# Expert tiles of a mixture-of-experts layer: pad slots are left out of the gathers and of the result writes, and the results go to token order

## The chip, the core and the metric

One core of one Trainium2 chip runs the whole program. The metric is the device time of one execution in microseconds (us), as the median of several executions.

## The reference, cut to what matters

Two layers of a transformer trunk work on 384 tokens (128 of a prompt, 256 latent ones) of width 1024, all in float32. Each layer has a token-mixing half (four parallel mixers, gates, projections) and then a mixture of experts. Only the second is touched by the change:

```python
scores = jax.nn.sigmoid((t @ lp['w_router']).astype(jnp.float32))
...
_, eidx = lax.top_k(masked, TOP_K)                 # 4 of 32 experts for each token
w = jnp.take_along_axis(scores, eidx, axis=-1)
w = w / jnp.sum(w, axis=-1, keepdims=True) * ROUTE_SCALE
combine = jnp.sum(jax.nn.one_hot(eidx, N_EXPERTS, dtype=jnp.float32) * w[..., None], axis=1)
gu = jnp.einsum('nd,edf->nef', t, lp['w_exp_gu'])
a = jax.nn.silu(gu[..., :EXPERT_FF]) * gu[..., EXPERT_FF:]
a = (a * combine[..., None].astype(a.dtype)).reshape(-1, N_EXPERTS * EXPERT_FF)
routed = a @ lp['w_exp_down'].reshape(N_EXPERTS * EXPERT_FF, D_MODEL)
```

A shared expert is added for every token, and the sum goes through an RMS norm, a gate and a residual add.

## The kernel before

A loop over the two layers holds one block in which every engine has its own program; semaphores tie them together. Data of the expert stage:

- 384 tokens choose 4 experts each: 1536 choices (`CHOICES`), 48 for an expert on average. Choices are laid out in *tiles* of `CAP` = 96 slots that belong to one expert. There are `NT` = 48 tiles at most; an expert with more than 96 choices gets a second one. The trace has 64 tiles over two layers, so each expert has one. Half of the slots of a layer's 32 tiles hold no choice; they are *pads*.
- The number of a slot is worked out for each choice on VectorE (`slot_u`, 12 columns: 3 token blocks times 4 choices). GpSimd scatters the token numbers to a table in DRAM, `slot_tokens`, by 12 indirect DMAs (L823), and reads it back whole into SBUF as `tokens` (L826). A table constant fills the pads with the numbers 0 to 95, so a pad fetches a real row that nobody needs.
- For each tile GpSimd copies one column of the table to `index` (L833) and issues an indirect DMA that gathers 96 rows of 4 KB from `token_rows` to `xg` (L836). Two tile buffers alternate (`e` = 0, 1).
- TensorE, for one step of a tile (the loop `steps`): transposes the rows of the tile two ahead (L1940), gate-and-up product of the tile one ahead (L1670, 16 matmul records), transposes the activated product of its own tile (L1903), and down product of its own tile (L1670, 8 records). ScalarE (L1175 to L1185) and VectorE (L1638, L1566, L1643) empty PSUM. The results land in `yrow`.
- SyncE (SP) issues the weights of the experts, 2 MB (L657) and 1 MB (L660) for each tile, and `write_rows` (L689): 96 rows of 4 KB to `y_slots`, at the slots' places, pads included. ScalarE and VectorE wait on `y_written` before they fill the same `yrow` buffer again, two tiles later.
- After the last tile GpSimd waits for both `y_written` and gathers the results by 12 indirect DMAs of 128 rows (L856), one for each token block and choice, into six buffers `ybuf`. VectorE adds each to `acc` with its weight (L1652), and after each fourth one (the next block's second is done first) runs the norm and residual of a block (`residual`, L1493 to L1495). The next layer starts behind that.
- Slots beyond tile 32 are zeroed ahead of time: a memset (L800) and a 6 MB DMA from GpSimd (L802), in the gate stage.

Every chunk of the layer runs in the order in which it is written for its engine; nothing is scheduled at run time. Two places are serial for the whole core: the hand-over from routing to the first tile (VectorE, 12 scatters, table, gather, TensorE), and the end of a layer (last result, write, gathers, sums).

## Time and profile before

| what | value |
|---|---|
| time, median of 3 runs | 2414.11 us (2413.77 to 2420.31) |
| profiled execution: first to last instruction | 2406.7 us |
| median time less that span | 7.4 us |
| TensorE busy | 2112.7 us (88%) |
| VectorE / ScalarE / GpSimd busy | 843.8 / 641.6 / 283.2 us |
| DMA moved | 455.49 MB, 189 GB/s over the span |
| DMA issues in the expert stage | 64 of 2 MB, 64 of 1 MB, 64 result writes of 384 KB, 64 gathers |

The profiled execution has no time of its own beside its span; the 7.4 us are what a run has outside its first and last instruction. Busy time is a share of the whole span, and the stages differ much. In the expert stages (about 770 to 1167 us and 1970 to 2361 us from the start) both TensorE and the DMA engines show tenths of 9 and above, so which of the two sets the pace has to be read from what TensorE waits for.

### The profile page before, as it was taken

Reading aid. Unit: us, or ns where it says so; the run is one execution under the profiler, and the core shown is the slowest. Engines: PE = TensorE matmul, PEld = TensorE weight load, DVE = VectorE, ACT = ScalarE, POOL = GpSimd, SP = SyncE. Lnnn points to the kernel's source line nnn. Section 1 sums busy time; section 2 is a strip of 40 time slices with the busy share of each in tenths; the row PEclk is TensorE's granted clock in tenths of the full one; section 3 lists DMA queues with packets and bytes.
Section 4 is the critical chain, followed back from the end, with each engine's and each line's share of the span. In section 5 each row is a group of like instructions: output and inputs, shape, how many; then the busy total and the mean of one; then the engine's idle time right before and its main releaser. Section 6 shows DMA issues by size and latency. Waiting matters only on the chain. (4 is left out here: it accounts for less than half of the span.)

```text
span 2406.7 us, 24752 instructions
## 1 busy us (share of the span) xinstructions
PE 2112.7 (88%) x8386; PEld 1283.7 (53%) x8386; DVE 843.8 (35%) x1476; ACT 641.6 (27%) x1330; POOL 283.2 (12%) x318
## 2 busy tenths in 40 slices
PE   6999898999976999999379998989999769999992
PEld 1298666788763333333113886667887523333330
DVE  0224466544444111111412345665444531111114
ACT  1133246433240111111111332474333401111111
POOL 0000420400003000000200006104000020000002
PEclk9999999999987999999789999999999889999996
DMA  9643210363333799999495432104533439999984
GB/s 312 224 138 127 84 36 1 104 206 123 131 132 105 271 329 326 328 327 321 163 310 192 150 124 74 36 1 150 178 123 114 154 92 313 326 331 322 332 292 168
DMA packets 205619, 455.49 MB, mean 189 GB/s; under 512 B 18668, under 2 KB 29260, under 8 KB 205524
## 3 DMA queue, kind: packets, MB, share of 16 engines
q1 hardware_dynamic: 174592, 384.86, 46.9%
q0 software_dynamic: 17216, 58.84, 7.3%
q10 hardware_dynamic: 13720, 10.60, 1.4%
q8 instruction: 54, 0.88, 0.2%
q14 instruction: 37, 0.30, 0.0%
HBM read 409.63 MB, written 44.68 MB: 189 GB/s over the span
## 5 line engine op out<-in xcount | busy, mean ns | idle before, releaser
L1670 PE MATMUL psum<-W,zf 128*96 128x512 f32 (+1 forms) x1584 | 715.1, 601 | 43.8 <-ACT zf L1181 41.0
L1670 PEld LDWEIGHTS psum<-W,zf 128*96 128x96 f32 (+1 forms) x1584 | 251.9, 166 | 413.0 <-issue 356.0
L1718 PE MATMUL psum<-W_split,qT_split 128*128 128x512 f32 (+3 forms) x1536 | 410.4, 379 | 6.9 <-ACT hT L909 6.6
L1268 DVE TENSOR_TENSOR W_split<-W,W_split 128x2048 fp32r<-128x2048 f32 (+3 forms) x96 | 221.3, 2307 | 428.1 <-ACT W_split L937 428.1
L1718 PEld LDWEIGHTS psum<-W_split,qT_split 128*128 128x128 f32 x1536 | 283.9, 189 | 62.5 <-ACT hT L909 7.3
L937 ACT ACTIVATE W_split<-W 128x2048 fp32r<-128x2048 f32 (+3 forms) x96 | 175.7, 1838 | 489.5 <-PE psum L1718 360.3
L1718 PE MATMUL psum<-W_split,scratch_split 128*128 128x512 f32 x864 | 281.0, 397 | 0.7 <-DVE hT_split L1263 0.7
L1670 PE MATMUL psum<-W,silT 128*2 128x512 f32 x384 | 169.9, 605 | 76.6 <-DMA W<-in_w_mod 76.6
L1718 PE MATMUL psum<-W_split,hT_split 128*128 128x512 f32 x576 | 214.8, 400 | 5.8 <-DVE scratch_split L1456 5.8
L1718 PEld LDWEIGHTS psum<-W_split,scratch_split 128*128 128x128 f32 x864 | 162.4, 189 | 39.8 <-DVE hT_split L1263 1.1
L1566 DVE TENSOR_TENSOR zf<-psum,zf 96x256 f32<-96x256 f32 x64 | 26.9, 421 | 433.8 <-ACT zf L1179 416.7
L1718 PE MATMUL psum<-W_split,kT_split 128*128 128x512 f32 (+3 forms) x480 | 177.3, 369 | 0.0
L1670 PEld LDWEIGHTS psum<-W,silT 128*2 128x2 f32 x384 | 32.8, 86 | 212.7 <-issue 207.4
L1179 ACT ACTIVATE zf<-psum 96x256 f32<-96x256 f32 x62 | 23.5, 379 | 419.8 <-PE psum L1670 419.8
L1718 PEld LDWEIGHTS psum<-W_split,hT_split 128*128 128x128 f32 x576 | 109.9, 191 | 32.1 <-DVE scratch_split L1456 6.3
L1643 DVE COPY zf<-psum 96x512 f32<-96x512 f32 x64 | 44.0, 687 | 236.4 <-PE psum L1670 236.4
L1718 PEld LDWEIGHTS psum<-W_split,kT_split 128*128 128x128 f32 x480 | 91.1, 190 | 14.9
L1670 PE MATMUL psum<-kT,qT 64*128 64x384 f32 (+3 forms) x288 | 90.7, 477 | 5.8 <-ACT qT L973 2.8
L1940 PEld LDWEIGHTS psum<-const,zf 96*128 96x128 f32 x512 | 52.0, 147 | 63.9 <-issue 38.1
L1940 PE MATMUL psum<-const,zf 96*128 96x96 f32 x512 | 56.4, 256 | 27.9 <-DMA zf<-token_rows,vm 22.7
L833 POOL COPY vm<-vm 96x1 uint32 (+1 forms) x64 | 11.5, 180 | 579.1 <-PE psum L1940 573.8
L1341 DVE TENSOR_REDUCE nmax<-psum 128x1 f32<-128x128 f32 (+1 forms) x144 | 65.0, 465 | 39.2 <-PE psum L1670 37.5
(280 smaller groups left out, 2067.8 us busy)
## 6 DMA issues: line engine op xcount, KB each, us to landing
W<-in_w_exp_gu SPq DMA_DIRECT2D x64, 2048.0 KB, 9.5
W<-in_w_exp_down SPq DMA_DIRECT2D x64, 1024.0 KB, 9.4
W<-in_w_in SPq DMA_DIRECT2D x60, 1024.0 KB, 5.0
W<-in_w_mod SPq DMA_DIRECT2D x24, 2048.0 KB, 9.8
y_slots<-zf SPq DMA_DIRECT2D x64, 384.0 KB, 9.5
W<-in_w_br SPq DMA_DIRECT2D x16, 1024.0 KB, 4.9
y_slots<-kT POOLq DMA_DIRECT2D x2, 6144.0 KB, 32.8
W<-in_w_out SPq DMA_DIRECT2D x8, 1024.0 KB, 4.9
```

Of the source, the lines that this page charges most:

```text
L833: nc.gpsimd.tensor_copy(index[0:CAP, e:e + 1], col).then_inc(S[f"index_copied{e}"], 1)
L937: nc.scalar.activation(high(j), piece(SPLITS[j]), ACT.Copy).then_inc(S["high_ready"], 1)
L1179: nc.scalar.activation(silu[0:CAP, 1 - e, :], psum[0:CAP, BANK_GU + 1 - e, 0:FF], ACT.Silu).then_inc(S["silu_ready"], 1)
L1268: V.tensor_tensor(piece(SPLITS[j], Wr), piece(SPLITS[j]), high(j).bitcast(F32), ALU.subtract).then_inc(S["low_ready"], 1)
L1341: V.tensor_reduce(nmax[:, col:col + 1], bank(key, P * len(keys_of(t))), AX, ALU.max, negate=True).then_inc(S["max_ready"], 1)
L1566: V.tensor_tensor(av[0:CAP, s], psum[0:CAP, gu, FF:2 * FF], silu[0:CAP, s], ALU.mult).then_inc(S["dve_emptied"], 1)
L1643: V.tensor_copy(yrow[0:CAP, e, C:], psum[0:CAP, BANK_Y + 1, :]).then_inc(S["dve_emptied"], 1)
L1670: ins = nc.tensor.matmul(dst, lhsT, rhs, start=(i == 0), stop=(i == len(pairs) - 1))
L1718: ins = nc.tensor.matmul(bank(job, piece_size(key)[1]), act_part[:, k0 + k, t * P:(t + 1) * P], w_part[:, k, :], start=first and (k, i) == ...
L1940: ins = nc.tensor.transpose(psum[:, BANK_XT + h, k * CAP:(k + 1) * CAP], xg[0:CAP, s, (4 * h + k) * P:(4 * h + k + 1) * P], ident[0:CAP, 0 ...
```

## The change

The table in DRAM now holds *places*: token number times 4 plus the choice's rank. A pad holds 262144. SBUF gets `places`, and VectorE makes `tokens` of it by a shift (262144 becomes 65536). The gather has `bounds_check` 383 and the result write is an indirect DMA with `bounds_check` 1535, both without an error, so a slot beyond the bound is left out. Results go to `y_rows` in token order, 4 rows of 4 KB for each token, and are read back as six plain DMAs of 1 MB, issued by SP: for a token block, two neighbouring rows of each token. The zeroing and its DMA are gone. `xg` is cleared once in each layer, since pads are no longer written. `y_written` gets its first count from two small DMAs to `y_spare`, where SP raised it before.

```diff
-        ybuf = zf[:, 7680:13824].rearrange("p (s n) -> p s n", s=6)
+        ybuf = zf[:, 7680:13824].rearrange("p (s k n) -> p s k n", s=3, k=2)
...
-        tokens = vm[:, 1068:1068 + NT].bitcast(U32)
+        place_f = vm[:, 1556:1568]
+        places = vm[:, 1068:1068 + NT].bitcast(U32)
         index = vm[:, 1120:1122].bitcast(U32)
+        place_u = vm[:, 1488:1500].bitcast(U32)
+        tokens = vm[:, 1500:1500 + NT].bitcast(U32)
+        place_index = vm[:, 1552:1554].bitcast(U32)
...
-                    def write_rows(turn, e, less=(0, 0)):
-
-                        sp.wait_ge(*job_emptied(turn, e, "y0", less[0]))
-                        sp.sem_inc(S["sp_steps"], 1)
-                        sp.wait_ge(*job_emptied(turn, e, "y1", less[1]))
-                        sp.sem_inc(S["sp_steps"], 1)
-                        dst = a["y_slots"].rearrange("(p i) n -> p i n", i=NT)[:, bass.ds(turn * 2 + e, 1), :].rearrange("p o n -> p (o n)")
-                        sp.dma_start(dst, yrow[0:CAP, e, :]).then_inc(S[f"y_written{e}"], 16)
...
@@ -700,13 +691,19 @@
                                 load_gate_up(1 - e, expert("w_exp_gu", expert_of(tile + 3)))
                             sp.wait_ge(*job_filled(turn, e, "y1"))
                             load_down(e, expert("w_exp_down", expert_of(tile + 2)))
-                            write_rows(turn, e)
 
                     with sp.Fori(0, turns - 2) as turn:
                         steps(turn)
                     steps(turns - 2, last=True)
                     for e in range(2):
-                        write_rows(turns - 1, e, (LESS["act"][e], LESS["dve"][e]))
+                        sp.wait_ge(S[f"y_written{e}"], turns * 16 + 16)
+                        sp.sem_inc(S["sp_steps"], 1)
+                    for i in range(T * TOPK // 2):
+                        if i >= 3:
+                            sp.wait_ge(S["summed"], 2 * (i - 2))
+                        t, k = divmod(2 * i, TOPK)
+                        src = a["y_rows"].rearrange("(t p k) n -> t p k n", t=T, k=TOPK)[t, :, k:k + 2, :]
+                        sp.dma_start(ybuf[:, i % 3], src).then_inc(S[f"y_landed{i % 3}"], 16)
...
-                    nc.gpsimd.memset(zero_row, 0.0).then_inc(S["zeros_ready"], 1)
-                    pool.wait_ge(S["zeros_ready"], 1)
-                    pool.dma_start(a["y_slots"].rearrange("(p i) n -> p i n", i=NT)[:, NE:, :],
-                                   zero_row[0:CAP, None, :].to_broadcast([CAP, NT - NE, D])).then_inc(S["zeros_out"], 16)
...
                     pool.wait_ge(*filled(("R", T - 1)))
                     nc.gpsimd.memset(ones, 1.0).then_inc(S["ones_ready"], 1)
+                    pool.wait_ge(S["ones_ready"], 1)
+                    for e in range(2):
+                        pool.dma_start(a["y_spare"][e:e + 1, :], ones[0:1, :]).then_inc(S[f"y_written{e}"], 16)
...
                     pool.wait_ge(*filled(("mgT", KD // 2)))
-                    pool.wait_ge(S["zeros_out"], 16)
...
                     for i in range(T * TOPK):
-                        pool.indirect_dma_start(a["slot_tokens"], bass.IndirectOffsetOnAxis(ap=slot_u[:, i:i + 1], axis=0),
-                                                token_u[:, i // TOPK:i // TOPK + 1], None).then_inc(S["slots_out"], 16)
+                        pool.indirect_dma_start(a["slot_places"], bass.IndirectOffsetOnAxis(ap=slot_u[:, i:i + 1], axis=0),
+                                                place_u[:, i:i + 1], None).then_inc(S["slots_out"], 16)
+                    nc.gpsimd.memset(xg[0:CAP], 0.0).then_inc(S["x_cleared"], 1)
                     pool.wait_ge(S["slots_out"], 16 * T * TOPK)
-                    pool.dma_start(tokens[0:CAP], a["slot_tokens"].rearrange("(p i) o -> p (i o)", i=NT)).then_inc(S["table_in"], 16)
-                    pool.wait_ge(S["table_in"], 16)
+                    pool.dma_start(places[0:CAP], a["slot_places"].rearrange("(p i) o -> p (i o)", i=NT)).then_inc(S["table_in"], 16)
+                    pool.wait_ge(S["x_cleared"], 1)
+                    pool.wait_ge(S["tokens_ready"], 1)
                     pool.wait_ge(S["rows_out"], 16 * T)
 
                     def gather(tile, e, n):
@@ -834,8 +830,24 @@
                         pool.wait_ge(S[f"index_copied{e}"], n)
                         pool.sem_inc(S["gathers"], 1)
                         pool.indirect_dma_start(xg[0:CAP, e, :], None, a["token_rows"],
-                                                bass.IndirectOffsetOnAxis(ap=index[0:CAP, e:e + 1], axis=0)).then_inc(S[f"x_landed{e}"], 16)
-
+                                                bass.IndirectOffsetOnAxis(ap=index[0:CAP, e:e + 1], axis=0),
+                                                bounds_check=T * P - 1, oob_is_err=False).then_inc(S[f"x_landed{e}"], 16)
+
+                    def scatter(turn, e, less=(0, 0)):
+
+                        pool.wait_ge(*job_emptied(turn, e, "y0", less[0]))
+                        pool.sem_inc(S["gathers"], 1)
+                        pool.wait_ge(*job_emptied(turn, e, "y1", less[1]))
+                        nc.gpsimd.tensor_copy(place_index[0:CAP, e:e + 1], places[0:CAP, bass.ds(turn * 2 + e, 1)]
+                                              ).then_inc(S[f"place_copied{e}"], 1)
+                        pool.wait_ge(S[f"place_copied{e}"], turn + 3)
+                        pool.sem_inc(S["gathers"], 1)
+                        pool.indirect_dma_start(a["y_rows"], bass.IndirectOffsetOnAxis(ap=place_index[0:CAP, e:e + 1], axis=0),
+                                                yrow[0:CAP, e, :], None,
+                                                bounds_check=CHOICES - 1, oob_is_err=False).then_inc(S[f"y_written{e}"], 16)
+
...
                             pool.wait_ge(*job_filled(turn, e, "xt1"))
                             gather(turn * 2 + e + 4, e, turn + 3)
-
+                            scatter(turn, e)
                     for e in range(2):
-                        pool.wait_ge(S[f"y_written{e}"], turns * 16 + 16)
-                        pool.sem_inc(S["gathers"], 1)
-                    for i in range(T * TOPK):
-                        if i >= 6:
-                            pool.wait_ge(S["summed"], i - 5)
-                        pool.indirect_dma_start(ybuf[:, i % 6, :], None, a["y_slots"],
-                                                bass.IndirectOffsetOnAxis(ap=slot_u[:, i:i + 1], axis=0)).then_inc(S[f"y_landed{i % 6}"], 16)
+                        scatter(turns - 2, e)
+                    for e in range(2):
+                        scatter(turns - 1, e, (LESS["act"][e], LESS["dve"][e]))
...
-                    for t in range(T):
-                        ins = V.tensor_scalar(token_f[:, t:t + 1], const[:, K_POS + 3:K_POS + 4], float(t * P), None, ALU.add)
+                    for i in range(T * TOPK):
+                        ins = V.tensor_scalar(place_f[:, i:i + 1], const[:, K_POS + 3:K_POS + 4], float(TOPK), float(i // TOPK * P * TOPK + i % TOPK),
+                                              ALU.mult, ALU.add)
                     link(ins)
-                    V.tensor_copy(token_u, token_f)
+                    V.tensor_copy(place_u, place_f)
                     V.tensor_copy(slot_u, slot_f).then_inc(S["slots_ready"], 1)
...
+                    dve.wait_ge(S["table_in"], 16)
+                    V.tensor_scalar(tokens[0:CAP], places[0:CAP], 2, None, ALU.logical_shift_right).then_inc(S["tokens_ready"], 1)
...
                     post_gains(1)
                     for i in range(T * TOPK):
-                        dve.wait_ge(S[f"y_landed{i % 6}"], 16 * (i // 6 + 1))
-                        V.scalar_tensor_tensor(acc[:, i // TOPK], ybuf[:, i % 6], weight[:, i:i + 1], acc[:, i // TOPK], ALU.mult,
+                        dve.wait_ge(S[f"y_landed{i // 2 % 3}"], 16 * (i // 6 + 1))
+                        V.scalar_tensor_tensor(acc[:, i // TOPK], ybuf[:, i // 2 % 3, i % 2], weight[:, i:i + 1], acc[:, i // TOPK], ALU.mult,
                                                ALU.add).then_inc(S["summed"], 1)
                         dve.wait_ge(S["summed"], i + 1)
...
-    no_tokens = np.ascontiguousarray(np.broadcast_to(np.arange(CAP, dtype=np.uint32)[:, None], (CAP, NT)))
+    no_places = np.full((CAP, NT), TOPK << 16, np.uint32)
...
-    a["y_slots"] = nc.dram_tensor("y_slots", (CAP * NT, D), F32, kind="Internal").ap()
-    a["slot_tokens"] = nc.dram_tensor("slot_tokens", (CAP * NT, 1), U32, kind="Internal").ap()
+    a["y_spare"] = nc.dram_tensor("y_spare", (2, P), F32, kind="Internal").ap()
+    a["y_rows"] = nc.dram_tensor("y_rows", (CHOICES, D), F32, kind="Internal").ap()
+    a["slot_places"] = nc.dram_tensor("slot_places", (CAP * NT, 1), U32, kind="Internal").ap()
```

On GpSimd's queue, the loop over turns and what follows it. Before (from the first tile of a turn; `zf` holds `xg` and `ybuf`, `vm` the index columns; ISA and REGISTER_ALU rows are waits and counters):

```order
L833 ISA
L833 COPY vm<-vm 96x1
L834 REGISTER_ALU
L836 DMA zf<-token_rows,vm 96x1024
L847 REGISTER_ALU
L833 ISA
L833 COPY vm<-vm 96x1
L836 DMA zf<-token_rows,vm 96x1024
L845 ISA
L845 COMPARE_AND_BRANCH
L851 ISA
L856 DMA zf<-y_slots,vm 128x1024 x12
```

The same place after:

```order
L829 ISA
L829 COPY vm<-vm 96x1
L830 REGISTER_ALU
L832 DMA zf<-token_rows,vm 96x1024
L838 ISA
L840 REGISTER_ALU
L841 ISA
L841 COPY vm<-vm 96x1
L845 DMA y_rows<-zf,vm 1536x1024
L859 REGISTER_ALU
L829 ISA
L829 COPY vm<-vm 96x1
```

A copy and an indirect write now stand between two gathers, behind waits for the emptied results of the tile.

On SP's queue, the end of a layer. Before:

```order
L660 DMA W<-in_w_exp_down 128x2x1024
L684 REGISTER_ALU
L686 REGISTER_ALU
L689 ISA
L689 DMA y_slots<-zf 96x1024
```

After:

```order
L662 DMA W<-in_w_exp_down 128x2x1024
L699 ISA
L706 DMA zf<-y_rows 128x2048 x6
L627 UNCONDITIONAL_BRANCH
```

The writes have left SP, and the six reads stand behind its wait for them.

On VectorE's queue, ahead of the signal `slots_ready` (the second CAST) that GpSimd's scatters wait for. Before:

```order
L1598 TENSOR_REDUCE vm<-zf 128x12
L1600 TENSOR_SCALAR vm<-const 128x1 x3
L1602 CAST vm<-vm 128x3
L1603 CAST vm<-vm 128x12
L1606 TENSOR_TENSOR zf<-psum,zf 128x256 x3
```

After:

```order
L1607 TENSOR_REDUCE vm<-zf 128x12
L1609 TENSOR_SCALAR vm<-const 128x1 x12
L1612 CAST vm<-vm 128x12
L1613 CAST vm<-vm 128x12
L1616 TENSOR_TENSOR zf<-psum,zf 128x256 x3
```

Nine small instructions are new there.

## Rows read from the trace of the kernel before

**Rows 1.** The page's first line.

```profile
span 2406.7 us, 24752 instructions
```

**Rows 2.** Chain that ended last, layer 2: start us, us, what.

```profile
1984.97 6.88 PE psum L1670 x16
...
2333.30 6.88 PE psum L1670 x16
...
2361.70 3.01 DMA y_slots<-zf
```

**Rows 3.** Timeline of one tile step: start, us, engine, instruction [idle before <- releaser].

```profile
2100.91 0.38 SPq L657 DMA_DIRECT2D W<-in_w_exp_gu  x1
...
2104.91 7.03 PE L1670 MATMUL psum<-W,zf 128*96 128x512 f32 x16
...
2105.25 0.18 POOL L833 COPY vm<-vm 96x1 uint32 x1 [10.06 <-PE psum L1940]
...
2106.24 0.92 POOL L836 DMA_INDIRECT zf<-token_rows,vm  x1 [0.80 <-POOL vm L833]
...
2112.80 3.67 PE L1670 MATMUL psum<-W,zf 128*96 128x512 f32 x8 [0.69 <-ACT zf L1181]
...
2116.60 0.69 DVE L1643 COPY zf<-psum 96x512 f32<-96x512 f32 x1 [3.79 <-PE psum L1670]
```

**Rows 4.** Windows: stretch, its us, busy by engine (instructions), clock, DMA share, GB/s.

```profile
2100.00:2196.00 96.00, 90.85 (x274) 38.02 (x272) 12.85 (x24) 13.45 (x32) 8.85 (x16) 1.00 0.95 325
...
1180.00:1190.00 10.00, 0.00 (x0) 0.00 (x0) 9.01 (x8) 2.73 (x4) 6.83 (x6) 0.50 0.97 370
...
2365.00:2400.00 35.00, 0.00 (x0) 0.00 (x0) 23.25 (x21) 5.62 (x10) 13.30 (x12) 0.51 0.51 180
```

**Rows 5.** DMA issues: count, KB each, median us from issue to landing.

```profile
W<-in_w_exp_gu SPq DMA_DIRECT2D x64, 2048.0 KB, 9.5
...
W<-in_w_br SPq DMA_DIRECT2D x16, 1024.0 KB, 4.9
...
zf<-token_rows,vm POOLq DMA_INDIRECT x64, 8.7
```

**Rows 6.** Timeline from routing to the first tile, layer 2.

```profile
1942.39 0.28 DVE L1600 TENSOR_SCALAR vm<-const 128x1 f32<-128x1 f32 x3
...
1960.37 0.59 POOL L826 DMA_DIRECT2D vm<-slot_tokens  x1 [1.46 <-DMA slot_tokens<-vm]
...
1965.87 0.96 POOL L836 DMA_INDIRECT zf<-token_rows,vm  x1 [0.85 <-POOL vm L833]
...
1970.04 1.54 PE L1940 MATMUL psum<-const,zf 96*128 96x96 f32 x8 [10.84 <-DMA zf<-token_rows,vm]
...
1973.73 8.30 PE L1670 MATMUL psum<-W,zf 128*96 128x512 f32 x16
```

**Rows 7.** The same place in layer 1.

```profile
765.65 0.58 POOL L826 DMA_DIRECT2D vm<-slot_tokens  x1 [3.16 <-DMA slot_tokens<-vm]
...
776.66 9.50 PE L1670 MATMUL psum<-W,zf 128*96 128x512 f32 x16
```

**Rows 8.** The line of the memset: ns min/median/max, first and last start.

```profile
L800 POOL MEMSET kT<- x2: 956/960/964, 470.8 to 1665.7; 128x1024 f32 x2
```

**Rows 9.** Chain that ended last, while the zeroing DMA ran (first) and behind it.

```profile
1636.03 50.58 PE psum L1718 x216
1687.91 50.32 PE psum L1718 x216
```

**Rows 10.** Timeline of the end of layer 2.

```profile
2360.37 0.69 DVE L1643 COPY zf<-psum 96x512 f32<-96x512 f32 x1 [3.55 <-PE psum L1670]
...
2365.53 0.97 POOL L856 DMA_INDIRECT zf<-y_slots,vm  x1 [54.15 <-DMA y_slots<-zf]
...
2369.95 1.28 DVE L1652 SCALAR_TENSOR_TENSOR zf<-zf,vm 128x1024 f32<-128x1024 f32 x1 [6.63 <-DMA zf<-y_slots,vm]
...
2390.48 2.60 DVE L1652 SCALAR_TENSOR_TENSOR zf<-zf,vm 128x1024 f32<-128x1024 f32 x2
```

More of the change, by code:

```diff
@@ L368, in trunk @@
                  "lam_dots", "lam_exps", "head_normed", "mean_ready", "ret_squared", "branch_rs"]
-        names += ["gates_out", "gates_in", "cache_out"] + [f"{n}{i}" for n in ("x_landed", "y_written", "index_copied") for i in range(2)]
-        names += [f"y_landed{i}" for i in range(6)]
-        names += ["dec_scaled", "mixture_rows", "post_root", "pre_root", "zeros_ready", "zeros_out", "halves_used", "high_ready", "low_ready", "h_split", "oT_high", "mgT_high"]
+        names += ["gates_out", "gates_in", "cache_out"] + [f"{n}{i}" for n in ("x_landed", "y_written", "index_copied", "place_copied") for i in range(2)]
+        names += [f"y_landed{i}" for i in range(3)]
+        names += ["dec_scaled", "mixture_rows", "post_root", "pre_root", "x_cleared", "tokens_ready", "halves_used", "high_ready", "low_ready", "h_split", "oT_high", "mgT_high"]
         landed_names = [f"mod_landed{i}" for i in range(SLOTS)] + [f"piece_landed{i}" for i in range(RAW)] + ["gu_landed0", "gu_landed1", "dn_landed0", "dn_landed1"]
@@ L2022 @@
     consts, earlier, lam_init = constants()
[L2024 removed]
+    no_places = np.full((CAP, NT), TOPK << 16, np.uint32)
     arrays = {name: np.ascontiguousarray(inputs[name]) for name in INPUTS}
[L2026 to L2027 removed]
+    arrays.update(consts=consts, earlier=earlier, lam_init=lam_init, no_places=no_places)
+    a = {name: nc.dram_tensor(f"in_{name}", v.shape, U32 if name == "no_places" else F32, kind="ExternalInput").ap() for name, v in arrays.items()}
     a["gate_rows"] = nc.dram_tensor("gate_rows", (2, 2, D), F32, kind="Internal").ap()
     a["token_rows"] = nc.dram_tensor("token_rows", (T * P, D), F32, kind="Internal").ap()
[L2030 to L2031 removed]
+    a["y_spare"] = nc.dram_tensor("y_spare", (2, P), F32, kind="Internal").ap()
+    a["y_rows"] = nc.dram_tensor("y_rows", (CHOICES, D), F32, kind="Internal").ap()
+    a["slot_places"] = nc.dram_tensor("slot_places", (CAP * NT, 1), U32, kind="Internal").ap()
     a["outs"] = {name: nc.dram_tensor(f"out_{name}", shape, F32, kind="ExternalOutput").ap() for name, shape in OUTPUTS}
```

10 lines of the change are left out of this document (3 added, 7 removed).

## The prediction

> **What bounds the kernel now.** I read the page first for the span [rows 1], then the chain that ended last, then the timeline of one tile step, and last the two places where the chain leaves TensorE.
>
> The chain through an expert stage is nothing but TensorE's gate-and-up and down products. One step of a tile takes 12.01 us: the gate-and-up runs of layer 2 start at 1984.97 and 2333.30, 29 steps apart [rows 2]. Within a step TensorE runs 7.03 us and 3.67 us back to back with its transposes, and the wait ahead of the second run, 0.69 us, ends with a ScalarE copy [rows 3]. Over eight steps it is busy 90.85 of 96 us at full clock [rows 4]. The DMA engines look just as full, 0.95 at 325 GB/s. The question is whether TensorE ever waits for them. It does not: the 2 MB load issued at 2100.91 lands after about 9.5 us [rows 5], at 2110.4, and the product that reads it starts one step behind the 7.03 us run of 2104.91, at about 2116.9 [rows 3]. That leaves 6.5 us. A gather is issued at 2106.2, lands after 8.7 us, and is transposed two steps after the issue, near 2128: 13 us to spare. So the DMA engines are full because TensorE's pace asks for about that many bytes, and fewer bytes buy nothing there.
>
> What remains are two serial places in each layer. From the routing to the first tile TensorE sits idle for 10.84 us and waits for a gather [rows 6]. At the end of a layer VectorE waits for results: the last one is emptied at 2361.06 (2360.37 plus 0.69), the first sum starts at 2369.95, and the last two sums end at 2393.08 [rows 10].
>
> **The change, part by part.**
>
> *Steady steps: 0 us.* Bytes per step fall by half of two times 0.39 MB, 0.39 MB in all. Hidden by TensorE, as above. GpSimd gets one copy and one indirect write for each tile; it is busy 8.85 of 96 us [rows 4], so issue time is no matter. The wait is: the write stands ahead of the next gather. The result of a tile is emptied at 2117.3 (2116.60 plus 0.69), the copy takes 0.18 and the gap behind it 0.8 (the gather's copy starts at 2105.25, and the gather itself about 1.0 later) [rows 3], the issue about 0.95. The next gather, which would have gone out at 2118.3, goes out near 2120.4. That is 2 us of 13. The buffer `yrow` is asked for again two steps (24 us) after its filling, against some 1 us to the issue and 8.7 us to land [rows 5]: 14 us to spare. Without this cover each microsecond of delay would cost 62 us over both layers; I see nothing that uses it up. SP loses an issue for each tile, which nobody waited for.
>
> *Zeroing removed: 0 to -0.3 us a layer.* The 6 MB DMA ran behind the memset at 1665.7 [rows 8], beside a stretch of 216 matmuls that took 50.58 us; the next such stretch without it took 50.32 us [rows 9]. I take -0.1 a layer.
>
> *Routing to first tile: +0.9 us in layer 1, +1.4 us in layer 2.* VectorE runs nine more instructions ahead of `slots_ready`; three take 0.28 us [rows 6], so nine are +0.84 us. GpSimd clears `xg` behind the last table scatter: 1024 columns take 0.96 us [rows 8], so 2048 take 1.9 us. It waits there for the scatters to land anyway, 3.16 us in layer 1 [rows 7] and 1.46 us in layer 2 [rows 6]: 0 and +0.46 us. The shift on VectorE is a new stop between table and first gather. An instruction of its size is 0.1 to 0.3 us, and a hop from VectorE to another queue costs between nearly nothing and the 0.64 us that SP needs from 2361.06 to its issue at 2361.70 [rows 2, 10]; so 0.1 to 0.9 us, and I take +0.4, nearer to the low end because the next instruction is a plain copy and no DMA issue. The first gather takes 4.17 us from its start to TensorE's first transpose (1965.87 to 1970.04) [rows 6]. Its 0.39 MB are 1.2 us at 325 GB/s [rows 4]; with half of the rows, 0.6 us less if pads lie evenly on the DMA engines, nothing if one engine still has a full share. I take -0.3.
>
> *End of a layer: +0.2 us each.* Before, 8.89 us pass from the last emptied result to the first sum. After: about 0.2 us to the copy, 0.2 for it, 0.8 behind it [rows 3], then the indirect write. Its landing the trace does not show. The near rows are the plain write of the same rows, 3.01 us [rows 2], and the indirect gather, 4.17 us; the far one is a gather in full traffic, 8.7 us [rows 5]. I take 4.0, since traffic is over by then. SP adds 0.64 us, and a plain 1 MB read lands after 4.9 us [rows 5]. Sum 1.2 + 4.0 + 0.64 + 4.9 = 10.7 us, +1.85 us.
>
> Some of that comes back. The run of sums took 23.13 us (2369.95 to 2393.08). VectorE was busy 23.25 us to the very end, of which 12 sums of 1.28 us are 15.4 [rows 4, 10]; the other 7.9 us are three residuals of 2.6, the third behind the run. So the run holds 20.6 us of work and 2.5 us of waits. Afterwards the reads follow each other at 2.83 us for 1 MB, at the 370 GB/s that the engines gave in this stretch [rows 4], against 2.60 us for two sums [rows 10]; two pairs wait 0.2 us, then a residual gives slack. The fourth read, issued when the first pair is summed, can land at 13.4 us from the start of reading and is asked for at about 15.8. With 0.3 us of gaps between instructions the run is 21.4 us, -1.7 us. At 325 GB/s it would be -1.0.
>
> A rule of the Trainium skill speaks to the 4.9 us. "DMA: Bandwidth & Descriptors", section "Anatomy of one DMA", gives a DMA a fixed part of about 2.0 us, mostly the receipt of the write, plus its bytes at 436 GB/s; an estimate from this page is 4.4 us for 1 MB. The row shows 4.9 from issue to landing, half a microsecond more. By the page the total would be 2415.6, by the row it is 2416.6. The same section calls HBM the slowest target for that receipt, and the scattered write now stands ahead of all the reads; that it costs more here no run has shown.
>
> **The sum.** Start +0.9 and +1.4, ends 2 times +0.2, zeroing 2 times -0.1: +2.5 us. The profiled span of 2406.7 us becomes 2409.2; the median has 7.4 us outside the span, so 2414.1 becomes 2416.6 us. A measurement of this kernel tells differences over about 0.3%, 7.2 us.
>
> **The rivals.**
>
> *The DMA engines set the pace after all (faster).* For it: share 0.95 in the steady stretch. Then half of the pads' bytes, 0.39 MB at 325 GB/s, gives 1.2 us a step, 62 steps, -75 us: 2340 us. It would decide where loads land later than 16 us from their issue; they land after 9.5. Chance 0.07, which also holds any smaller gain over 0.3%.
>
> *Indirect DMAs with a bound cost GpSimd more (slower).* No row has one. On the path of each layer stand one gather at the start and one write at the end, four in all. It decides from 1.2 us more for each (4.7 us over four). At three times the present 0.92 us it is +7.4 us: 2424 us. Against it: a comparison for each row is little beside building a descriptor. Chance 0.09.
>
> *The three queued reads share the engines (slower).* If the first three 1 MB reads progress side by side, the first lands with the third, near 4.9 + 2 times 2.83 = 10.6 us instead of 4.9. VectorE then never waits again, so it is +5.2 us a layer: 2427 us. Against it: six gathers were in flight before, and the first landed after 4.4 us [rows 10]. It decides from 7.3 us for the first. Chance 0.06.
>
> *Pads are not really left out.* If their rows still move, only the -0.3 a layer is lost: 2417.2 us. This lies inside my forecast.
>
> **How the numbers follow.** Forecast (no measurable change) 0.78, faster 0.07, slower 0.09 + 0.06 = 0.15. Unknowns around the forecast: the start from +0.3 to +2.2 us a layer, the end from -1.5 (write lands as the plain one, read a little earlier) to +3 us. TensorE's clock behind its long wait adds some: the first 16 products take 9.50 us in layer 1 and 8.30 in layer 2, where 7.03 is the rule [rows 3, 6, 7], and a shifted restart may fall either way, -3.7 to +1.2 us together. That gives 2408 to about 2425; taken to the rivals on the slow side, 2427.
>
> **What would show each step.** In the changed trace: steps still 12.0 us apart with the wait ahead of the down product still on ScalarE; DMA share in the steady stretch down from 0.95 to near 0.86 at about 292 GB/s; the GpSimd indirect instructions still near 0.95 us; the gathers about 2 us later in each step; 0.5 to 1.5 us more from `slots_ready` to the first transpose; first sum 10 to 11 us behind the last emptied result, and sums without waits over 0.3 us after that. A step other than 12.0 us, a bounded DMA over 2 us, or a first read over 7 us would make me wrong.

## The result, and the profile after

| | median | runs | ratio to before (95%) |
|---|---|---|---|
| before | 2414.17 us (2404.12 to 2424.13) | 20 | |
| after | 2420.77 us (2415.28 to 2429.95) | 20 | 1.0029 [1.0017, 1.0040] |

The ratio is +7.0 us (4.1 to 9.7): a small loss, just under the 7.2 us that I had called the limit of what can be told from no change. The forecast was 2416.6 us.

The profiled execution of after was its slowest: 2429.95 us with a span of 2428.1. Set against the 2406.7 us of [rows 1] that is 21.4 us, three times what the medians show. The stages below are therefore compared mostly between a later pair of executions of the same two kernels, `c_before` (span 2404.2) and `c_after` (2413.0).

From the page of after: the span, and three DMA issues (count, KB, median us to landing).

```profile
span 2428.1 us, 24890 instructions
...
W<-in_w_exp_gu SPq DMA_DIRECT2D x64, 2048.0 KB, 8.4
W<-in_w_exp_down SPq DMA_DIRECT2D x64, 1024.0 KB, 7.8
...
zf<-y_rows SPq DMA_DIRECT2D x12, 1024.0 KB, 7.3
```

The view of DMA issues has the two indirect ones:

```profile
zf<-token_rows,vm POOLq DMA_INDIRECT x64, 6.0
y_rows<-zf,vm POOLq DMA_INDIRECT x64, 7.1
```

The 2 MB loads land after 8.4 us, 9.5 before [rows 5] (9.1 in `c_before`), and the gathers after 6.0 instead of 8.7. The DMA engines have more room, but the steady steps of TensorE are no shorter. The window of [rows 4], of after (busy by engine PE, PEld, DVE, ACT, POOL; then clock, DMA share, GB/s):

```profile
2100.00:2196.00 96.00, 90.85 (x273) 38.02 (x272) 12.85 (x24) 13.45 (x32) 18.44 (x32) 1.00 0.84 290
```

TensorE's busy time is the same 90.85 us as in [rows 4], to the last digit shown. The DMA share fell from 0.95 to 0.84, the rate from 325 to 290 GB/s. Two steps of the chain of after, 29 steps apart:

```profile
2003.16 6.88 PE psum L1682 x16
...
2351.50 6.88 PE psum L1682 x16
```

(2351.50 - 2003.16) / 29 is 12.01 us a step, as before. One step of after in the timeline (start, us, engine, instruction, idle before and what ended it):

```profile
2106.97 3.67 PE L1682 MATMUL psum<-W,zf 128*96 128x512 f32 x8 [0.69 <-ACT zf L1190]
2107.04 0.38 SPq L659 DMA_DIRECT2D W<-in_w_exp_gu  x1
...
2110.77 0.69 DVE L1655 COPY zf<-psum 96x512 f32<-96x512 f32 x1 [3.79 <-PE psum L1682]
...
2111.14 7.03 PE L1682 MATMUL psum<-W,zf 128*96 128x512 f32 x16
...
2111.38 0.54 DVE L1650 COPY zf<-psum 128x384 f32<-128x384 f32 x1
...
2111.63 0.18 POOL L841 COPY vm<-vm 96x1 uint32 x1 [8.10 <-ACT zf L1184]
...
2112.70 0.94 POOL L845 DMA_INDIRECT y_rows<-zf,vm  x1 [0.89 <-POOL vm L841]
...
2114.71 0.99 POOL L832 DMA_INDIRECT zf<-token_rows,vm  x1 [0.86 <-POOL vm L829]
```

The down product still waits 0.69 us for ScalarE. The result is emptied at 2111.46, the copy of the index starts at 2111.63, the scatter at 2112.70, the next gather at 2114.71. No instruction of TensorE waits for any of this. GpSimd's copy takes 0.18 us here although it runs beside a VectorE copy out of PSUM (L1650).

The start of the expert stage in layer 2, in the timeline of after:

```profile
1959.80 0.82 DVE L1609 TENSOR_SCALAR vm<-const 128x1 f32<-128x1 f32 x12
...
1976.95 1.82 POOL L819 MEMSET zf<- 96x2048 f32 x1
...
1978.70 0.56 POOL L821 DMA_DIRECT2D vm<-slot_places  x1
1982.99 0.18 DVE L1638 TENSOR_SCALAR vm<-vm 96x48 uint32<-96x48 uint32 x1 [5.10 <-DMA vm<-slot_places]
...
1984.53 1.04 POOL L832 DMA_INDIRECT zf<-token_rows,vm  x1 [0.93 <-POOL vm L829]
...
1988.44 1.54 PE L1952 MATMUL psum<-const,zf 96*128 96x96 f32 x8 [11.28 <-DMA zf<-token_rows,vm]
```

Twelve place instructions take 0.82 us where three took 0.28 [rows 6]. The clearing of `xg` (1.82 us) runs behind the last scatter, and the shift (0.18 us) stands between the table's landing and the first index copy.

The end of layer 2, in the chain of after that ended last:

```profile
2378.56 0.70 DVE zf L1655
...
2379.42 2.15 POOL vm L841
...
2381.70 0.73 issue
2382.43 3.31 DMA y_rows<-zf,vm
...
2385.83 5.54 DMA zf<-y_rows
...
2391.47 1.29 DVE zf L1664
```

The lines are, in order, the stops from the last result to the first sum. The line to look at is the second: GpSimd needs 2.15 us for a copy of 96 numbers. The timeline of the same place shows what ran beside it, and how the layer ended:

```profile
2379.17 2.35 DVE L1495 TENSOR_TENSOR kT<-kT 128x1024 f32<-128x1024 f32 x2
2379.42 2.14 POOL L841 COPY vm<-vm 96x1 uint32 x1 [2.23 <-DVE zf L1655]
...
2391.47 7.89 DVE L1664 SCALAR_TENSOR_TENSOR zf<-zf,vm 128x1024 f32<-128x1024 f32 x6 [9.95 <-DMA zf<-y_rows]
...
2410.20 2.60 DVE L1664 SCALAR_TENSOR_TENSOR zf<-zf,vm 128x1024 f32<-128x1024 f32 x2
...
2415.92 1.23 DVE L1504 TENSOR_TENSOR x<-x,zf 128x1024 f32<-128x1024 f32 x1
```

VectorE multiplies two pairs of SBUF tiles (L1495, 2.35 us from 2379.17) while GpSimd copies from 2379.42. The same products stood at this place before; GpSimd had nothing to do there then. A milder sign was in the trace of before, a few us later, in its timeline:

```profile
2368.06 0.93 POOL L856 DMA_INDIRECT zf<-y_slots,vm  x1 [0.30 <-issue]
...
2369.95 1.28 DVE L1652 SCALAR_TENSOR_TENSOR zf<-zf,vm 128x1024 f32<-128x1024 f32 x1 [6.63 <-DMA zf<-y_slots,vm]
2370.54 1.51 POOL L856 DMA_INDIRECT zf<-y_slots,vm  x1 [0.30 <-issue]
```

A gather's issue took GpSimd 0.93 us with VectorE idle and 1.51 us beside a sum, which also reads two tiles in SBUF. Not each issue beside a sum was longer (1.01 us at 2376.76), but of the twelve gathers of this layer none without VectorE beside it took over 0.97 us.

The differences by stage, each worked out from starts and ends of instructions in the traces (us; layer 1 / layer 2):

| stretch | `c_before` | `c_after` |
|---|---|---|
| start of the span to layer 1's router | 708.69 | 710.34 |
| router's first product to first table scatter | 38.28 / 38.25 | 38.83 / 38.81 |
| to the table's load | 16.64 / 16.58 | 16.93 / 16.96 |
| to the first gather | 5.02 / 5.34 | 5.15 / 5.50 |
| to TensorE's first transpose | 4.19 / 4.10 | 3.70 / 3.84 |
| first transpose to last result emptied | 391.38 / 391.15 | 391.15 / 390.79 |
| last result emptied to first sum | 8.77 / 8.86 | 11.93 / 11.93 |
| run of the sums | 23.09 / 23.02 | 21.34 / 21.34 |
| last result emptied to last residual's end | 36.20 / 36.24 | 37.61 / 37.61 |
| last residual's end to the next layer's first product | 16.37 | 16.31 |
| layer 2's first product to its router | 686.5 | 688.5 |
| last residual's end to the end of the span | 9.2 | 10.9 |

The starts cost 0.5 and 0.8 us, the ends of layers 1.4 each, the end of the program 1.7: together +5.8 us. The last was on no list of mine. The expert stages gave back 0.2 and 0.4 us, nearly all of it ahead of the third tile's gate-and-up product (the first 16 products took 8.31 / 7.88 us, before 8.48 / 8.43); from there on the steps are alike. The two spans differ by 8.8 us. The remaining 3.6 us lie in the first and the last but one row (1.7 and 2.0), where the change touches no more than the zeroing and two small DMAs, and where executions differ widely whatever the kernel: the stretch to layer 2's router took 685.8 to 691.5 us in the kernels made of before and 687.0 to 691.3 in those made of after.

### The profile page after: what moved, and what is told of

Read it like the earlier page. It is cut to its first block and busy times, and to the rows that moved or that the text cites. A ratio compares the mean times of both kernels' runs of the same rounds, so it can differ in the third digit from the quotient of the medians.

```text
span 2428.1 us, 24890 instructions
## 1 busy us (share of the span) xinstructions
PE 2126.8 (88%) x8386; PEld 1294.8 (53%) x8386; DVE 847.4 (35%) x1496; ACT 642.5 (26%) x1330; POOL 338.4 (14%) x424
## 2 busy tenths in 40 slices
DMA packets 200910, 417.73 MB, mean 172 GB/s; under 512 B 24716, under 2 KB 35308, under 8 KB 199284
## 5 line engine op out<-in xcount | busy, mean ns | idle before, releaser
L841 POOL COPY vm<-vm 96x1 uint32 x64 | 15.3, 239 | 512.5 <-ACT zf L1184 469.4
```

## The experiments

The kernels ran on three chips, each beside runs of before on the same chip (medians of before 2412.2, 2410.8 and 2412.6 us). Ratios are to those. None of the kernels leaves out or changes part of the computation; the gathers of `e4_gather_only` leave out pads, as those of after do.

**1. The two kernels again** (`c_before`, `c_after`), for the stages above.

> The kernel before again, unchanged, to see what its stages do from run to run. Theory A: serial distances as before (last result emptied to first sum 8.8 us, VectorE's sums 23.1 to 23.4 us), while the distance from router to first table scatter moves by up to 5 us between runs with the granted clock; ratio to itself 1.000 within 0.003. Rival B (the change slows routing): that distance stays at 36.6 to 38.3 us in both layers.

> The changed kernel again, unchanged, for a second profile. Theory A: of the 21 us between the two profiled spans (2406.7 and 2428.1) only 5 us belong to the change, 1.5 us at each layer's end and 1.0 us at each start; the rest is TensorE's granted clock falling to 0.61 for some 10 us in the routing stage of each layer (router to first table scatter 42.1 us in both layers, where the kernel before took 36.6 and 38.3). Then this profile shows the same serial distances (last result emptied to first sum 12.0 to 12.2 us, table load to first gather 5.5 to 5.8) but another routing stage, 37 to 42 us. Rival B: the change itself slows the routing stage; then it is again 42 us in both layers. Median 2416 to 2424.

Measured: 2411.49 us, ratio 0.9997 [0.9980, 1.0014], and 2421.10 us, ratio 1.0036 [1.0019, 1.0053]. The routing took 38.8 us in both layers of `c_after`, so the rival that the change itself slows it to 42 us falls. The +1.4 us at each layer's end is there in both pairs of traces.

**2. VectorE's two products moved away from the copy** (`e1_port`): they run before the first tile.

```diff
                     for i in range(2):
                         empty(("xt", i, 1), xT[:, i, 4:8].rearrange("p k n -> p (k n)"), psum[:, BANK_XT + 1, 0:4 * CAP])
+                    post_gains(1)
                     product(BANK_GU, 0, T + 1)
...
                     steps(turns - 1, last=True)
 
-                    post_gains(1)
                     for i in range(T * TOPK):
```

> The changed kernel with VectorE's two products of gate and gain (128x1024 each, two SBUF inputs, 2.35 us together) taken from the layer's end to the start of the tile loop, where VectorE waits anyway. Theory A: in the changed kernel GpSimd's 96x1 copy of the last scatter's indices starts 0.2 us behind these products and takes 2.14 us in place of 0.18, ending with them, because the two engines do not reach SBUF together; with the products gone the copy is 0.18 us, the last result write goes out 1.96 us sooner in each layer, last emptied result to first sum falls from 12.2 to about 10.3 us, and the median by 3.9 us to about 2417. Rival B: the copy is late because it waits for its register or for the scatter before it; then it stays at 2.1 us, and nothing changes. Rival C: the products only move their cost to the start; the first step gets 2.4 us longer.

The copies of L841 over the whole of `c_after`, by line (ns min/median/max, first and last start):

```profile
L841 POOL COPY vm<-vm x64: 177/178/2143, 802.4 to 2364.6; 96x1 uint32 x64
```

The same view of `e1_port`:

```profile
L841 POOL COPY vm<-vm x64: 177/178/181, 801.4 to 2360.0; 96x1 uint32 x64
```

At most 181 ns are left. The end of layer 2 in the timeline of `e1_port`:

```profile
2359.17 0.69 DVE L1656 COPY zf<-psum 96x512 f32<-96x512 f32 x1 [3.55 <-PE psum L1682]
2360.03 0.18 POOL L841 COPY vm<-vm 96x1 uint32 x1 [2.23 <-DVE zf L1656]
2361.08 0.93 POOL L845 DMA_INDIRECT y_rows<-zf,vm  x1 [0.87 <-POOL vm L841]
...
2369.77 5.25 DVE L1664 SCALAR_TENSOR_TENSOR zf<-zf,vm 128x1024 f32<-128x1024 f32 x4 [9.91 <-DMA zf<-y_rows]
```

The first sum starts 9.91 us behind the last emptied result (2359.86), where `c_after` has 11.93. From the emptied result to the last residual's end it is 35.54 / 35.61 us, 2.0 less than `c_after` and 0.65 less than `c_before`. At their new place the products lengthen nothing that TensorE waits for: its expert stages took 391.17 / 390.74 us (391.15 / 390.79 in `c_after`), though one gather's issue beside them took 1.47 us instead of 0.98. Total 2413.90 us, ratio 1.0013 [0.9995, 1.0031]; I had expected about 2417. So the clash is shown: the scattered results alone make a layer's end shorter, and the copy beside the products made it longer. It isn't VectorE's activity as such that holds the copy: 58 of the 64 copies of L841 ran inside a VectorE copy out of PSUM, and each took 0.18 us.

**3. The first read in two halves** (`e2_split`).

```diff
+                        if i == 0:
+                            for j in range(2):
+                                sp.dma_start(ybuf[:, 0, j], src[:, j, :]).then_inc(S[("y_landed0", "y_second")[j]], 16)
+                            continue
```

> The changed kernel with the first of the six reads cut in two halves of 512 KB, each with its own semaphore. Theory A: the first sum starts when half of the bytes are there, 1.4 us sooner (512 KB at 370 GB/s), so first read issue to first sum falls from 5.6 to about 4.3 us; VectorE then waits a little more for the next pair (0 to 1 us), so 0.4 to 1.4 us a layer in all. Rival B: three reads in flight share the engines and the first lands late for that reason; then halves of the first land hardly earlier, by less than 0.5 us.

2419.58 us, ratio 1.0029 [1.0012, 1.0045]. The first sum came 1.4 us sooner (3.98 us behind the read's issue, 5.35 before), but the run of sums grew from 21.34 to 23.0: the later reads land no sooner (the second pair 8.2 us behind the first read's issue, 7.7 in `c_after`), and the wait only moved. From the last emptied result to the last residual's end it is 37.94 us, 0.3 more than `c_after`. A miss.

**4. Twice the result writes** (`e3_more_writes`, made of before): does TensorE or DMA set the pace?

```diff
+                        again = a["y_again"].rearrange("(p i) n -> p i n", i=NT)[:, bass.ds(turn * 2 + e, 1), :].rearrange("p o n -> p (o n)")
+                        sp.dma_start(again, yrow[0:CAP, e, :]).then_inc(S[f"y_written{e}"], 16)
                         sp.dma_start(dst, yrow[0:CAP, e, :]).then_inc(S[f"y_written{e}"], 16)
```

> The kernel before, with every result write issued twice by SP, the second copy to a DRAM tensor that nobody reads: 0.39 MB more for each step, as much as the change takes away. Theory A (TensorE sets the pace of the steady steps): the step stays 12.01 us, or grows by less than 0.2, while the DMA engines move about 357 GB/s; only the layer's end gets about 1 us longer. Rival B (the DMA engines set it): the step grows by 1.2 us, 75 us in all.

The window of [rows 4] in this kernel:

```profile
2100.00:2196.00 96.00, 90.86 (x274) 37.97 (x273) 12.84 (x24) 13.46 (x32) 8.85 (x16) 1.00 1.02 362
```

The DMA engines moved 362 GB/s at a share of 1.02, TensorE's busy time is 90.86 us, and the steps are 12.01 us as before. 2411.62 us, ratio 1.0009 [0.9992, 1.0026]. The first sum came about 1 us later in each layer (9.84 / 9.75 us behind the last emptied result), as expected. Adding bytes costs the steady steps nothing, so DMA doesn't set their pace, and taking bytes away could give nothing.

**5. Pads left out of the gathers alone** (`e4_gather_only`, made of before, with `xg` cleared).

```diff
-                                                bass.IndirectOffsetOnAxis(ap=index[0:CAP, e:e + 1], axis=0)).then_inc(S[f"x_landed{e}"], 16)
+                                                bass.IndirectOffsetOnAxis(ap=index[0:CAP, e:e + 1], axis=0),
+                                                bounds_check=T * P - 1, oob_is_err=False).then_inc(S[f"x_landed{e}"], 16)
```

> The kernel before with one part of the change alone: pads hold 65536 and are left out of the gathers by a bound, xg is cleared once a layer; writes, zeroing and the last twelve gathers are as before. Theory A: the step stays 12.01 us; first gather issue to the first transpose falls from 4.2 to 3.8 us, a bounded indirect DMA takes GpSimd 0.99 us instead of 0.93, and the memset costs 0.3 us ahead of the table load; together 0 within 1 us: skipping pads in the gathers is worth nothing here. Rival: the DMA engines' relief shortens the steps, up to 0.6 us each.

2411.39 us, ratio 0.9999 [0.9976, 1.0022]. The first gather reaches the transposes after 3.65 / 3.93 us (4.19 / 4.10 in `c_before`); the steady stretch has a DMA share of 0.89 and steps of 12.01 us. Leaving the pads out of the gathers is worth nothing here.

**6. Places worked out early** (`e5_early_places`): the twelve instructions and their cast go ahead of a VectorE wait for the router's tables.

```diff
+                    for i in range(T * TOPK):
+                        ins = V.tensor_scalar(place_f[:, i:i + 1], const[:, K_POS + 3:K_POS + 4], float(TOPK), float(i // TOPK * P * TOPK + i % TOPK),
+                                              ALU.mult, ALU.add)
+                    link(ins)
+                    V.tensor_copy(place_u, place_f)
                     dve.wait_ge(*emptied(("place",)))
```

> The changed kernel with the twelve place instructions and their cast ahead of VectorE's wait for the counts. Theory A: in the changed kernel they cost 0.56 us net (router to first table scatter 38.8 us instead of 38.3) and the cast for the tokens before was already in the path, so this distance falls to about 38.0 us, and the median by 1.5 to 2 us. Rival: VectorE has no idle time there and the distance stays.

The stretch from the router to the first scatter took 37.84 us in layer 1, 1.0 less than `c_after`; in layer 2, at the lower clock of point 9 below, it took 41.11 us, 1.0 less than the 42.11 of after at that clock. 2416.71 us, ratio 1.0021 [1.0003, 1.0039]: of this size the total can't tell.

**7. The end of the block: GpSimd's drain.** Every engine ends the block of a layer with a drain, and all wait for the last. The line of the drains in `c_before`, GpSimd's (POOLq) and VectorE's (ns min/median/max, first and last start):

```profile
L625 POOLq DRAIN  x2: 6107/6108/6108, 1196.3 to 2390.9; - x2
...
L625 DVEq DRAIN  x2: 1264/1264/1264, 1199.2 to 2393.7; - x2
```

The same line in `c_after`:

```profile
L627 POOLq DRAIN  x2: 7822/7822/7823, 1199.6 to 2398.0; - x2
...
L627 DVEq DRAIN  x2: 1261/1261/1261, 1202.5 to 2400.8; - x2
```

VectorE's last drain in `c_after` ends at 2400.8 + 1.26 = 2402.1, GpSimd's at 2398.0 + 7.82 = 2405.8. The block ends with GpSimd's, 3.7 us behind the last arithmetic; in `c_before` the same sum gives 2.0. GpSimd issues 74 DMAs in a layer before and 95 after (12 result gathers and the zeroing gone, 32 result writes and 2 small ones added): 6107 / 74 and 7822 / 95 are both 82 ns for each. The drain starts where GpSimd's wait for the twelfth sum passes. Three kernels test it. `e7_drain` is after without that wait (nothing on GpSimd needs it), `e8_before_drain` is before without it:

```diff
                     pool.wait_ge(S["cache_out"], 16 * 8)
-                    pool.wait_ge(S["summed"], T * TOPK)
```

> The changed kernel without GpSimd's wait for the twelve sums at the end of a layer. The profiles show that GpSimd then runs a drain instruction, 6.11 us long in the kernel before and 7.82 us in the changed one, that starts when the sums are done and ends last of all engines; the barrier to the next layer waits for it. Theory A: the drain costs 82 ns for each DMA that GpSimd issued in the layer (74 before, 95 after), and the 20 additional indirect writes are therefore paid a second time, 1.7 us at the end of the program and partly at the end of layer 1. Without the wait the drain runs behind the last write, hidden by the sums: last residual to the output DMA falls from 5.2 us to about 1.6 us, and the median by 3.5 to 7 us to about 2415. Rival B: the drain waits for something else that ends at that time (the outputs of other engines); then it still ends 3.8 us behind the residual.

> The kernel before without GpSimd's wait for the twelve sums. Theory A: its drain, 6.11 us for 74 DMAs, starts behind its last gather, some 9 us earlier, and is hidden; last residual to output DMA falls from 3.5 to about 1.6 us, the median by 2 to 4 us to about 2409. Rival B (the drain is not bound to the number of DMAs): no change.

`e10_more_dmas` is before with 21 small GpSimd DMAs in each layer's gate stage, far from the end:

```diff
+                    for i in range(21):
+                        pool.dma_start(a["spare"][i:i + 1, :], ones[0:1, :]).then_inc(S["extra_out"], 16)
```

> The kernel before with 21 small DMAs of 512 bytes more from GpSimd in each layer, issued in the gate stage where GpSimd waits for up to 177 us. Theory A (the drain costs 82 ns for each DMA that GpSimd has issued in the layer): the drain grows from 6.11 to 7.83 us although these DMAs landed long ago, and the last residual to the output DMA from 3.5 to 5.2 us; the median grows by 1.7 to 3.4 us. Rival B (only indirect DMAs, or only late ones, count): the drain stays at 6.11 us.

The drain of `e10_more_dmas`:

```profile
L625 POOLq DRAIN  x2: 7822/7822/7823, 1205.7 to 2410.1; - x2
```

The count alone gives the 7.82 us of after, wherever in the block the DMAs stand. The end of the span comes 10.9 us behind the last residual (9.2 in `c_before`), and the next layer's first product 18.48 us behind it (16.37): in the kernel before, 21 more DMAs cost 1.7 us at the end of the program and 2.1 at the end of layer 1. The total is 2415.31 us, ratio 1.0019 [1.0004, 1.0034]. Without the wait the drain starts 34.6 us ahead of the last residual's end in `e7_drain` (4.1 us in `c_after`) and is hidden: 7.2 us from the last residual to the end of the span, 12.21 to the next layer's first product (16.31 in `c_after`); total 2413.61, ratio 1.0015 [1.0000, 1.0030]. In `e8_before_drain` they are 7.3 and 14.56; total 2409.20, ratio 0.9988 [0.9972, 1.0003], an interval that still holds 1.

The 82 ns hold only for a drain that starts behind the wait for the sums. Started early, it was longer: 8.82 us for the same 95 DMAs in `e7_drain`, all of them landed, and 11.27 / 10.18 us for 74 in `e8_before_drain`, where the last gathers were still in flight. Why it grows I did not test.

**8. All three repairs** (`e9_port_early_drain`): after with the edits of 2, 6 and `e7_drain`.

> The changed kernel with three edits: the products of gate and gain at the start of the tile loop, the twelve place instructions and their cast ahead of VectorE's wait for the counts, and no GpSimd wait for the sums. Theory A adds 3.9 us for the products, 2 times 0.8 us for the places (router to first table scatter 38.0 us instead of 38.8) and 3.5 to 7 us for the drain: a median of 2409 to 2412, 0 to 5 us under the kernel before. Rival: the three overlap and give less than 8 us together.

Its drain, in the same view:

```profile
L627 POOLq DRAIN  x2: 8815/8816/8816, 1173.2 to 2364.4; - x2
```

It starts at 2364.4, behind the last result write, and ends some 26 us before the last residual does. 2405.84 us, ratio 0.9981 [0.9965, 0.9998]: 4.6 us faster than before (0.5 to 8.4), the fastest of all kernels here. I had expected 2409 to 2412. It is the better form of the change. How much of the lead belongs to the change itself stays open: before without the wait has 0.9988, and the two intervals overlap.

**9. What made the first two traces 21.4 us apart.** Set side by side by the stretches of the table, the routings took 10.4 us more in the trace of after (1.3 of them are the change's), the two stretches ahead of the routers 9.5 us more, the ends of the layers 2.6, the end of the program 1.7; the rest, -2.8 us, is mostly the first two steps of layer 1, slower in the trace of before. For the routing there is no kernel of its own: the router of layer 2 in two executions of the changed kernel shows it. Windows of after (the clock is the third number from the right):

```profile
1915.00:1925.00 10.00, 9.71 (x63) 9.71 (x63) 2.08 (x3) 3.31 (x5) 0.00 (x0) 0.71 0.13 52
1925.00:1935.00 10.00, 10.00 (x23) 5.52 (x23) 6.94 (x31) 1.53 (x2) 0.00 (x0) 0.61 0.40 159
```

TensorE's timeline there, the router's product and the shared expert's:

```profile
1919.64 7.62 PE L1682 MATMUL psum<-wr,hT 128*128 128x32 f32 x48
1927.07 23.69 PE L1682 MATMUL psum<-W,hT 128*128 128x512 f32 x48
```

The windows of the same place in `c_after`:

```profile
1905.00:1915.00 10.00, 10.00 (x72) 9.37 (x71) 2.74 (x5) 3.33 (x5) 0.00 (x0) 0.84 0.02 8
1915.00:1925.00 10.00, 10.00 (x21) 4.31 (x20) 9.52 (x31) 1.67 (x2) 1.59 (x3) 0.86 0.48 185
```

And its timeline:

```profile
1908.54 5.44 PE L1682 MATMUL psum<-wr,hT 128*128 128x32 f32 x48
1913.82 22.54 PE L1682 MATMUL psum<-W,hT 128*128 128x512 f32 x48
```

With the same instructions on TensorE, the granted clock was 0.71 and 0.61 in the one execution and 0.84 and 0.86 in the other, a mix of the two levels of 1.2 and 2.4 GHz. In both, TensorE had been idle shortly before, for 9.5 us and then for 2.5 to 2.8 us, with short transposes between. The two products took 7.62 and 23.69 us in the one, 5.44 and 22.54 in the other: 3.3 us. The stretch from the router to the first scatter shows 38.3 or 41.6 us in kernels with the routing of before too (`e8_before_drain` and `e10_more_dmas` both 41.6 in both layers, `c_before` 38.3; once, in layer 1 of the profiled execution of before, 36.6). The long form stands in 5 of 12 layers of the kernels made of before and in 4 of 14 of those made of after, so it comes by chance of the execution, and the change doesn't make it more frequent in these traces.

Over the 20 runs of after, time and mean clock of a run have a correlation of -0.92. This bears on the total too. The mean clock was 0.9444 over the 12 runs of `c_after` and 0.9471 over the 35 of before beside them. Read along the line that those 35 runs give, `c_after` is 4.5 us slower at equal clock, and some 4 us come with its lower clock. Longer waits at 1.2 GHz lower the mean by themselves: an estimate from 5.8 us of them is 0.001 of the 0.0027. Whether the rest is chance or the change's doing no run here shows.

## Why the prediction held, and where its sum was off

The range held the median, and the likeliest case (no measurable change) came in, near its edge. The predicted time was 4.2 us short. That the range held it is in part luck: the sum said +2.5 us, the measurement +7.0 (4.1 to 9.7), and only the room left for a measurable change took in the difference. By its own steps:

- *Steady steps: 0.* Right, and for the reason given: steps of 12.01 us, DMA share 0.84 (0.86 forecast), 290 GB/s (292), the gather about 2 us later. `e3_more_writes` shows it from the other side. The rival that DMA sets the pace falls.
- *Zeroing: -0.1 a layer.* No run shows it. The 50.58 us of [rows 9] had been laid to the zeroing DMA, but that DMA was in flight from 1667.0 to 1700.0, beside both stretches. The first stretch took 50.59 us in `c_after`, which has no such DMA, and 50.31 in `e4_gather_only`, which has it. The term is 0 as far as is known, and the reading of those rows was wrong.
- *Routing to first tile: +0.9 and +1.4.* It was +0.5 and +0.8. Nine more instructions +0.55 (forecast 0.84; the pipelined ones cost 60 ns each); clearing `xg` +0.3 and +0.4 (0 and 0.46); the shift +0.15 (0.4, mis-sized: the copy starts 0.16 us behind VectorE's result at the end of a layer, and 0.15 us is no more than the shift's own 0.18); the shorter gather -0.5 and -0.3 (-0.3). Between executions of one kernel the way from table to gather differs by up to 0.4 us (5.15 and 5.54 in layer 1), so the smallest of these are no firmer than that.
- *End of a layer: +0.2 each.* It was +1.4; this is the step that failed. In the line "about 0.2 us to the copy, 0.2 for it" the copy took 2.15. The price of the instruction was taken from a row where nothing contended with it [rows 3]: VectorE ran no more than a copy out of PSUM beside it, and what VectorE runs at that very place was not looked at, nor the longer gather issues beside VectorE's sums in the trace of before (1.51 us instead of 0.93). The other terms came out at 0.16 to the copy, 0.86 behind it, 3.31 for the write (4.0), 0.09 for SP (0.64), 5.54 for the read (4.9): without the clash they give 10.2 us to the first sum, and `e1_port` has 9.9. The run of sums took 21.34 us, forecast 21.4.
- *Missing: the drain.* I counted GpSimd's new DMAs for their issue time and not for what each leaves to the end of the block: +1.7 us at the end of the program. At the end of layer 1 it is there too, but the next layer's first product did not come later (16.31 and 16.37 us). SP's next instruction comes 3.0 to 3.1 us behind the loop's branch in the traces of before and 0.25 us behind it in those of after, and the first weight load behind it then lands about 1 us slower, which together hides the longer drain there. In `e10_more_dmas`, with the kernel of before around it, nothing hides it. Why SP's gap at the branch differs I did not test; it stays open.
- *Landing of the scattered write.* 3.31 us with the traffic over, near the plain write's 3.01 [rows 2]. The section "Anatomy of one DMA" of the Trainium skill's "DMA: Bandwidth & Descriptors", which the prediction set beside its 4.9 us, is about DMAs that GpSimd issues, while these reads are SP's. The row was the better source; with two reads queued behind it the first took 5.54 us.
- *The rivals.* A bounded indirect DMA costs 0.94 to 0.99 us on GpSimd, not three times 0.92. The first queued read lands after 5.5 us, not 10.6, though its 0.6 us over the forecast and the second pair of `e2_split` show that the reads do overlap a little. "Pads are not really left out" falls: 417.73 MB were moved instead of 455.49, with fewer bytes in the steady stretch. The 37.8 MB are what the pads' rows in gathers and writes (25.2) and the zeroing (12.6) come to.
- *The 7.4 us outside the span.* Wrong, and with it the base of the sum. The time of a run stands 1.85 us over its span (2429.95 and 2428.1; 2414.79 and 2413.0). The profiled execution of before was then a run of about 2408.6 us, 5.5 under the median; I took luck of the clock for a constant. As the forecast only added a difference to the median, it did no harm to the number.

The located differences are +5.8 us, or +5.2 with the expert stages, and the runs say +7.0 (4.1 to 9.7). The rest is within the interval; the clock of point 9 may have a part in it, which isn't shown.

## What to carry to other kernels

Before a cheap instruction is put on a serial path, look at what the other engines run in that very microsecond: a copy of 0.18 us may cost 2.1 beside VectorE operations with two SBUF inputs, and still 0.18 beside a VectorE copy out of PSUM. Count the DMAs that GpSimd issues in a block for its end too, and let GpSimd end its part of the block as early as its data allow. And where bytes are hidden behind TensorE, saving them gives nothing; what decides is what the saving puts onto the serial places.

## What the hardware showed that I had not expected

- GpSimd's copy of 96 x 1 numbers took 0.18 us 62 times and 2.14 us both times that VectorE multiplied 128x1024 tiles from SBUF beside it. It ended with the second product (2381.52 and 2381.56), as if held for both. By the Trainium skill, "GPSIMD Engine Reference", section "Specifications", GpSimd shares its SBUF interfaces with VectorE, with contention against an instruction that has two SBUF inputs; the trace agrees, and adds the size.
- The issue of an indirect DMA took GpSimd 0.93 to 0.99 us beside an idle VectorE in the trace of before, and up to 1.9 us beside VectorE's sums.
- GpSimd's drain behind its last wait took 82 ns for each DMA that it had issued in the block, though they had landed before: 6.11 us for 74, 7.82 us for 95. Started earlier it took longer, 8.82 us for 95.
- A lower granted clock behind the waits of the routing costs 3.3 us in one layer of one execution and nothing in another, more than several terms of this sum.
